# Attention of a two-layer hybrid backbone: transposed probabilities on three rotating PSUM banks, values in one piece at the head of odd steps

## The chip, the cores and the metric

The kernel runs on one core of one Trainium2 chip. The metric is the device time of one execution in microseconds, median over several; less is better. Of the core's engines, PE does the matrix products and transpositions, DVE is the vector engine, ACT the scalar engine, POOL the general-purpose one. Each engine works through its own queue in order, and semaphores tie the queues together: an instruction that waits holds up all that stand behind it in its queue.

## What is computed

Two layers, each with a SwiGLU feed-forward half step, a token mixing, and a second half step. The change touches only the attention inside the token mixing. Its core in the reference is, for 8 latent-attention heads ("mla") over all 768 tokens and 4 neighbourhood heads ("na") with a learned bias over a window:

```python
def attend(q, k, v, scale):
    s = jnp.einsum('bqhd,bkhd->bhqk', q, k).astype(jnp.float32) * scale
    p = jax.nn.softmax(s, axis=-1).astype(v.dtype)
    return jnp.einsum('bhqk,bkhd->bqhd', p, v)
...
    ya_x = blocked_attention(qa_x, jnp.concatenate([ka_c, ka_x], axis=1),
                             jnp.concatenate([va_c, va_x], axis=1), MLA_SCALE).reshape(B, S, MLA_WIDTH)
...
    yb_x = neighborhood_attention(qb_x, kb_x, vb_x, kb_c, vb_c, na_rpb, rows).reshape(B, S, NA_WIDTH)
```

There are 512 latent and 256 context tokens. A latent query attends to its latent keys (all 512, or the 256 or 384 near it in an na head) and the 256 context keys; a context query attends to the 256 context keys alone, and exists only in the first layer.

## The kernel before

Every matrix product is made of products of high and low parts in float32: an operand is split into a rounded part ("hi", written by ACT) and the rest ("lo", the difference, written by DVE or POOL). Feed-forward stages and projections keep PE busy for most of the span and are not touched. Attention is one stage in each layer, with its own loop on each engine: `attention_pe`, `attention_act`, `attention_dve` and `attention_pool`.

The unit of attention is a chunk of 128 queries of one head. Layer 0 has 72 chunks (each of 12 heads: 4 latent, 2 context), layer 1 has 48, all latent. The loops run over steps s. The work on one chunk c, and the step in which each engine's queue holds it, is:

- scores (PE, step c): matmuls into the PSUM tensor `pair[c % 2]`, lines L2086 to L2095.
- maximum (DVE, step c): one `tensor_reduce` over the scores, L2235.
- exponential (ACT, step c): from `pair` into `prob`, with the row sums, L2180.
- transposition of the probabilities (PE, step c + 2): 128x128 pieces into `pmid`, L2109. A latent chunk has two parts, the latent keys and the context keys, each with its own bank of `pmid`; a context chunk has the second part only. A part is written over only when the low half of the chunk before has been taken out of its bank.
- `pt_hi` (ACT, L2165) and `pt_lo` (DVE, L2254), both read from the transposed probabilities, step c + 2, one instruction for each part.
- values (PE, L2123 to L2136): for two chunks (2b, 2b+1) together, first two transpositions that spread the reciprocal sums, then matmuls of the values with `pt_hi` and `pt_lo`, into half of `psum2`. The first half of the matmuls stands in step 2b + 4, the second in 2b + 5, and pairs of chunks alternate between the two banks of `psum2`.
- read-out of the two chunks: a copy by ACT (L2173, step 2b + 5), a sum and a product by DVE (L2242 and L2244, step 2b + 6); the product's end is counted in `a_out`. A reciprocal (L2269) closes each even step on DVE.

ACT's queue in a step is: `pt_hi` of chunk s-2, the copy (odd s), the exponential of chunk s. Behind it, in the first three steps of a head, stands one splitting copy each for the next head (L2143). DVE's queue in a step is: maximum of chunk s, the two read-out instructions (even s), `pt_lo` of chunk s-2. PE's queue is: scores of s, both parts of the transposition of s-2, half of the values. The wait of the first half of the values lets two pairs be open:

```python
wait_if(eng, a_out, c0 // 2 + b - 1)
```

Of the kernel before, what the change touches and what calls it, by code (L numbers as in the profile page):

```python
# [29 lines left out]
P = 128  # L30
# [32 lines left out]
STATS = 6  # L63
# [138 lines left out]
def program(nc, x, c, ctx_in, c_ctx, w_mod, w_mod_rows, b_mod, w_gate, w_up, w_down, w_in, g_cq, w_q_up, g_ckv, w_kv_up,  # L202
            g_mla_q, g_mla_k, g_na_q, g_na_k, na_rpb, w_pool, pool_scale, w_out,
            k_ident, k_cos, k_sin, k_invcnt, out):
    with ExitStack() as ctx:
# [170 lines left out]
        a_latent_t, a_latent_hi, a_latent_lo = (sem(f"a_latent_{k}") for k in ("t", "hi", "lo"))  # L376
# [1661 lines left out]

        Y_ORDER = [0, 1, 6, 7, 2, 3, 4, 5]
# [23 lines left out]

        def attention_pe(eng, l):
# [6 lines left out]
            for s in range(n + 4):  # L2071
                if s == 2:
                    eng.wait_ge(v_free, TOK // P * (l + 1))
                if s < n:
                    kind, i, j, q0, keys = chunk_info(l, s)
                    g, new = att_group(l, s)
                    qh, ql, kh, kl = att_set[g % 2]
                    rows = slice(0, QK) if kind == "mla" else slice(0, 2 * NA_DIM)
                    if new:
                        eng.wait_ge(a_lo, ATT_SPLITS * l + splits(g)[0] + len(splits(g)[1]))  # L2080
                        if kind == "na":
                            eng.wait_ge(na_stacked, 48 * (NA_HEADS * l + g - MLA_HEADS + 1))
                    wait_if(eng, a_exp, c0 + s - 1)
                    for a, b in keys:
                        dst, q, d = pair[s % 2][:, a:b], slice(q0, q0 + P), moved(kind, q0, a)
                        eng.matmul(dst, qh[rows, q], kh[rows, a + d:b + d], start=True, stop=False)  # L2086
                        if kind == "mla":
                            eng.matmul(dst, qh[rows, q], kl[rows, a:b], start=False, stop=False)
                        last = eng.matmul(dst, ql[rows, q], kh[rows, a + d:b + d], start=False,
                                          stop=not (biased(l, s) and a < SEQ))  # L2090
                    if biased(l, s):
                        first, a = BIAS_FIRST[q0 // P], keys[0][0]
                        eng.wait_ge(bias_lo_done, bias_tables(l, s))
                        for table in (na_hi, na_lo):
                            last = eng.matmul(pair[s % 2][:, a:SEQ], ident_r[:, :], table[:, j, first:first + SEQ - a],  # L2095
                                              start=False, stop=table is na_lo)
                    last.then_inc(a_s, 1)
                if 2 <= s < n + 2:
                    c = s - 2
                    keys = chunk_info(l, c)[4]  # L2100
                    eng.wait_ge(a_exp, c0 + c + 1)
                    for a, b in keys:
                        part = a // SEQ
                        if part == 0:
                            wait_if(eng, a_latent_lo, latent_parts(l, c))
                        else:
                            wait_if(eng, a_ptl, c0 + c)
                        for k in range(a // P, b // P):
                            last = eng.transpose(pmid[:, k * P:(k + 1) * P], prob[:, c % 3, k * P:(k + 1) * P], ident[:, :])  # L2109
                        last.then_inc((a_latent_t, a_t)[part], 1)  # L2110
                if s >= 4:
                    b, part = (s - 4) // 2, s % 2
                    kind, i, j, q0, keys = chunk_info(l, 2 * b)
                    tiles = [[k for k in range(TOK // P) if k >= SEQ // P or 0 <= k - near(kind, x)[0] < near(kind, x)[1]]
                             for x in (q0, q0 + P)]
                    kc = sorted(set(tiles[0] + tiles[1]), key=lambda k: (k >= SEQ // P, not all(k in t for t in tiles), k))
                    if part == 0:
                        eng.wait_ge(a_ptl, c0 + 2 * b + 2)
                        wait_if(eng, a_out, c0 // 2 + b - 1)
                        eng.wait_ge(a_rsum, c0 + 2 * b + 2)  # L2120
                        for h in range(2):
                            at = (b % 2) * 512 + (2 + h) * P
                            eng.transpose(psum2[:, at:at + P], stat[:, (2 * b + h) % STATS, 2:3].broadcast_to([P, P]),  # L2123
                                          ident[:, :])
                    vals = v_both[:, :, 2 * i + j, :] if kind == "mla" else vn_both[i][:, :, j, :]
                    both = psum2[:, (b % 2) * 512:(b % 2) * 512 + 2 * P].rearrange("p (c q) -> p c q", c=2)
                    for k in kc[:len(kc) // 2] if part == 0 else kc[len(kc) // 2:]:
                        c1, c2 = [h for h in range(2) if k in tiles[h]][0], [h for h in range(2) if k in tiles[h]][-1] + 1
                        dst, slots = both[:, c1:c2, :], slice(2 * (b % 2) + c1, 2 * (b % 2) + c2)
# [365 lines left out]
```

## Time and profile before

| what | value |
|---|---|
| median of 3 runs | 2893.85 us (2892.34 to 2894.07) |
| the profiled execution, its own time | 2889.44 us |
| its span in the trace | 2887.6 us |
| PE busy over the span | 2807.2 us (97%) |
| DVE busy | 1482.7 us (51%) |
| ACT busy | 947.4 us (33%) |
| POOL busy | 263.3 us (9%) |

The trace is of one execution, which lies 4.4 us under the median of the runs. The shares are means over all stages: the feed-forward stages are PE's alone, and the attention stages, 813 to 987 us and 2334 to 2469 us of the span, are those in which PE, DVE and ACT all work most of the time.

### The profile page before, as it was taken

The numbers are of one execution on the slowest core, as the hardware profiler recorded it, in microseconds if no ns is written. First come the engines' busy times: TensorE is split into PE (matmuls) and PEld (weight loads), VectorE is DVE, ScalarE is ACT, GpSimd is POOL, SyncE is SP. The second block draws the span as 40 slices with busy tenths as digits, with TensorE's granted clock in tenths as the row PEclk, the third lists the DMA queues.
The fourth block names the chain that finished last, engine by engine and source line by source line (L and its number), as shares of the span: only waits on it lengthen the run. The fifth ranks groups of instructions, "written<-read, shape, count | busy, mean of one in ns | idle before, by whom it ended". The sixth has DMA issues, their size and how long they took to land.

```text
span 2887.6 us, 42480 instructions
## 1 busy us (share of the span) xinstructions
PE 2807.2 (97%) x16327; PEld 2646.7 (92%) x16327; DVE 1482.7 (51%) x2293; ACT 947.4 (33%) x1526; POOL 263.3 (9%) x279
## 2 busy tenths in 40 slices
PE   7999999999988899999999999999999998999999
PEld 5999999989977789999999999999998987888887
DVE  6554355455477665533553555245346587633332
ACT  3221122233388642211222322112224388532231
POOL 1000000031234210000000100000003234000000
PEclk9999999999999999999999999999999999999999
DMA  6433243223100224322442234133223201233333
GB/s 224 135 122 99 82 137 122 82 63 78 32 14 12 79 74 134 124 85 81 137 133 58 88 117 134 55 123 117 72 65 87 58 14 46 81 95 107 90 100 90
DMA packets 361092, 262.99 MB, mean 91 GB/s; under 512 B 11086, under 2 KB 339188, under 8 KB 359952
## 3 DMA queue, kind: packets, MB, share of 16 engines
q1 hardware_dynamic: 359440, 256.86, 29.5%
q10 hardware_dynamic: 896, 4.46, 0.4%
q8 instruction: 78, 1.28, 0.2%
q14 instruction: 38, 0.31, 0.0%
q0 software_dynamic: 640, 0.09, 0.0%
HBM read 255.08 MB, written 2.10 MB: 89 GB/s over the span
## 4 chain that ended last, share of the span: by engine, by line
PE 89%; ACT 4%; DVE 3%; issue 2%; POOL 1%; DMA 0%; SPq 0%; POOLq 0%; ACTq 0%; DVEq 0%
PE pair L427 24%; PE pair L428 24%; PE pair L435 24%; PE pair L1311 2%; PE pair L1313 2%; PE pair L1312 2%; PE pair L682 2%; PE pmid L2109 2%; PE pair L683 2%; PE pair L684 2%; ACT prob L2180 1%; ACT pt_hi L2165 1%; DVE pt_lo L2254 1%; PE psum L2134 1%; PE psum L2136 1%
## 5 line engine op out<-in xcount | busy, mean ns | idle before, releaser
L427 PE MATMUL pair<-h_lo,w_hi 128*128 128x384 f32 (+1 forms) x2656 | 906.4, 343 | 0.7 <-ACT sg L1102 0.4
L428 PE MATMUL pair<-h_hi,w_hi 128*128 128x384 f32 (+1 forms) x2656 | 905.4, 343 | 0.0
L427 PEld LDWEIGHTS pair<-h_lo,w_hi 128*128 128x128 f32 x2656 | 498.5, 188 | 22.8 <-issue 0.6
L428 PEld LDWEIGHTS pair<-h_hi,w_hi 128*128 128x128 f32 x2656 | 498.8, 188 | 21.3
L403 DVE TENSOR_TENSOR w_lo<-w_raw,w_hi 128x1024 fp32r<-128x1024 f32 (+1 forms) x262 | 349.0, 1332 | 324.5 <-ACT w_hi L396 321.3
L435 PE MATMUL pair<-h_hi,w_lo 128*128 128x384 f32 (+1 forms) x2656 | 513.8, 343 | 0.0
L435 PEld LDWEIGHTS pair<-h_hi,w_lo 128*128 128x128 f32 x2656 | 463.4, 188 | 20.6
L396 ACT ACTIVATE w_hi<-w_raw 128x1024 fp32r<-128x1024 f32 (+1 forms) x262 | 296.2, 1131 | 539.8 <-PE pair L435 507.4
L427 PE MATMUL pair<-s_lo,w_hi 128*128 128x384 f32 (+1 forms) x1100 | 377.7, 343 | 0.0
L428 PE MATMUL pair<-s_hi,w_hi 128*128 128x384 f32 (+1 forms) x1100 | 377.2, 343 | 0.0
L949 DVE SCALAR_TENSOR_TENSOR pmid<-mod_raw,cs_rows 128x1024 f32<-128x1024 f32 x256 | 315.3, 1232 | 74.8 <-DMA mod_raw<-in_w_mod_rows 58.1
L1133 DVE SCALAR_TENSOR_TENSOR xT<-pair,mv,xT 128x384 f32 (+4 forms) x160 | 76.5, 525 | 419.4 <-PE pair L435 415.0
L1106 ACT ACTIVATE s_hi<-sf 128x768 f32 (+3 forms) x88 | 69.8, 793 | 592.0 <-DVE sf L1160 592.0
L428 PEld LDWEIGHTS pair<-s_hi,w_hi 128*128 128x128 f32 x1100 | 206.5, 188 | 6.8
L427 PEld LDWEIGHTS pair<-s_lo,w_hi 128*128 128x128 f32 x1100 | 206.5, 188 | 6.8
L435 PE MATMUL pair<-s_hi,w_lo 128*128 128x384 f32 (+1 forms) x1100 | 209.4, 343 | 0.0
L670 POOL TENSOR_TENSOR h_lo<-nt,h_hi 128x256 fp32r<-128x256 f32 (+1 forms) x36 | 35.5, 985 | 1822.9 <-ACT nt L652 1822.9
L1102 ACT ACTIVATE sg<-pair 128x768 f32<-128x768 f32 (+1 forms) x88 | 66.9, 761 | 407.5 <-PE pair L435 407.5
L435 PEld LDWEIGHTS pair<-s_hi,w_lo 128*128 128x128 f32 x1100 | 193.8, 188 | 6.9
L1160 DVE TENSOR_TENSOR sf<-pair,sg 128x768 f32<-128x768 f32 (+1 forms) x88 | 78.4, 891 | 183.4 <-PE pair L435 178.9
L1162 DVE TENSOR_TENSOR s_lo<-sf,s_hi 128x768 f32 (+3 forms) x88 | 78.5, 892 | 91.3 <-ACT s_hi L1106 91.3
L2254 DVE TENSOR_TENSOR pt_lo<-pmid,pt_hi 128x512 fp32r<-128x512 f32 (+2 forms) x216 | 101.7, 507 | 31.4 <-ACT pt_hi L2165 29.8
(310 smaller groups left out, 3603.3 us busy)
## 6 DMA issues: line engine op xcount, KB each, us to landing
mod_raw<-in_w_mod_rows SPq DMA_DIRECT2D x64, 1024.0 KB, 4.9
w_raw<-in_w_ffn_gate SPq DMA_DIRECT2D x88, 512.0 KB, 3.8
w_raw<-in_w_ffn_up SPq DMA_DIRECT2D x88, 512.0 KB, 3.8
w_raw<-in_w_ffn_down SPq DMA_DIRECT2D x64, 704.0 KB, 4.6
w_raw<-in_w_in SPq DMA_DIRECT2D x32, 512.0 KB, 4.0
w_raw<-in_w_out SPq DMA_DIRECT2D x12, 512.0 KB, 4.2
w_raw<-in_w_q_up SPq DMA_DIRECT2D x8, 576.0 KB, 4.1
mod_first<-in_w_mod ACTq DMA_DIRECT2D x4, 1024.0 KB, 9.2
```

Of the source, the lines that this page charges most:

```text
L396: eng.activation(w_hi[:, t.odd, 0:w], raw[:, t.odd, 0:w], ACT.Copy).then_inc(w_hi_done, 1)
L403: eng.tensor_tensor(w_lo[:, t.odd, 0:w], raw[:, t.odd, 0:w], w_hi[:, t.odd, 0:w].bitcast(F32), ALU.subtract).then_inc(w_lo_done, 1)
L427: eng.matmul(dst, wh, rl, start=k == 0, stop=False)
L428: eng.matmul(dst, wh, rh, start=False, stop=False)
L435: last = eng.matmul(dst, wl, rh, start=False, stop=k == chunks - 1)
L949: eng.scalar_tensor_tensor(pmid[:, 0:D_MODEL], mod_raw[:, a, :], 1.0, cs_rows[:, j, :], ALU.mult, ALU.mult, accum_out=mod_out(v, a, j)).th ...
L1102: eng.activation(into, gate, ACT.Silu).then_inc(acc_free[o.odd], 1)
L1106: eng.activation(s_hi[:, bass.ds(i, 1), 0:w].rearrange("p a t -> p (a t)"), sf[:, 0:w], ACT.Copy).then_inc(s_hi_done, 1)
L1133: last = eng.scalar_tensor_tensor(xT[:, bass.ds(d, 1), a:b].rearrange("p a t -> p (a t)"), pair[o.odd][:, at:at + b - a], mv[:, 2, bass.ds ...
L1160: eng.tensor_tensor(into, up, gate, ALU.mult).then_inc(acc_free[(o + 1).odd], 1)
L1162: eng.tensor_tensor(s_lo[:, bass.ds(i, 1), 0:w].rearrange("p a t -> p (a t)"), sf[:, 0:w], s_hi[:, bass.ds(i, 1), 0:w].bitcast(F32).rearra ...
L2254: eng.tensor_tensor(pt_lo[:, (a + d) // P:(b + d) // P, c % 4, :], pmid[:, a:b].rearrange("p (k q) -> p k q", q=P), pt_hi[:, (a + d) // P: ...
```

## The change

The arithmetic stays the same. What moves is where results lie and the order of the queues:

- The transposed probabilities are numbered part by part, and part number x lies in one of three banks, x mod 3: the two of `pmid` and the second of `psum2`. A part may be written when the low half of the part three before has been taken.
- The values of all pairs go to the first bank of `psum2`, in one piece, at the head of odd steps (pair b in step 2b + 5). They wait until the read-out of pair b-1 is complete (`a_out` one higher than before).
- On PE the transposition of the latent part of chunk s-2 stands ahead of the scores of s, that of the context part behind them.
- On ACT the copy of the read-out stands behind the exponential, no longer ahead of it.
- On DVE `pt_lo` of the latent part stands ahead of the maximum, that of the context part behind it, and the read-out behind both.
- Three semaphores go; all parts count in `a_t`, `a_pth` and `a_ptl`.

```diff
--- before.py
+++ after.py
@@ new functions @@
+        def turn_no(l, c):
+
+            return ATT_C0[l] + c + latent_parts(l, c)
+
+        TURN_PLACES = [pmid[:, 0:512], pmid[:, 512:1024], psum2[:, 512:1024]]
+
+        def turned_at(number, a, b):
+
+            return TURN_PLACES[number % 3][:, 0:b - a].rearrange("p (k q) -> p k q", q=P)
...
+        def turn_part(eng, l, c, m):
+
+            keys = chunk_info(l, c)[4]
+            a, b = keys[m]
+            number = turn_no(l, c) + m
+            eng.wait_ge(a_exp, ATT_C0[l] + c + 1)
+            wait_if(eng, a_ptl, number - 2)
+            for k in range(a // P, b // P):
+                last = eng.transpose(turned_at(number, a, b)[:, k - a // P, :], prob[:, c % 3, k * P:(k + 1) * P], ident[:, :])
+            last.then_inc(a_t, 1)
+
+        def weigh_values(eng, l, b):
...
+            wait_if(eng, a_out, c0 // 2 + b)
+            eng.wait_ge(a_rsum, c0 + 2 * b + 2)
+            for h in range(2):
+                eng.transpose(psum2[:, (2 + h) * P:(3 + h) * P], stat[:, (2 * b + h) % STATS, 2:3].broadcast_to([P, P]),
+                              ident[:, :])
+            eng.wait_ge(a_ptl, turn_no(l, 2 * b + 2))
...
+            both = psum2[:, 0:2 * P].rearrange("p (c q) -> p c q", c=2)
+            for k in kc:
...
+            last.then_inc(a_pv, 1)
@@ attention_pe @@
             for s in range(n + 4):
                 if s == 2:
                     eng.wait_ge(v_free, TOK // P * (l + 1))
+                parts = len(chunk_info(l, s - 2)[4]) if 2 <= s < n + 2 else 0
+                if s >= 5 and s % 2:
+                    weigh_values(eng, l, (s - 5) // 2)
+                if parts == 2:
+                    turn_part(eng, l, s - 2, 0)
                 if s < n:
...
+                    attention_scores(eng, l, s)
+                if parts:
+                    turn_part(eng, l, s - 2, parts - 1)
@@ attention_act @@
-                if s >= 5 and s % 2 and s < n + 4:
-                    b = (s - 5) // 2
...
-                    eng.activation(y_f[r, i if kind == "mla" else 4 + i, q0:q0 + 2 * P], psum2[other, bank:bank + 2 * P],
-                                   ACT.Copy).then_inc(a_copied, 1)
                 if s < n:
...
-                    wait_if(eng, a_t, c0 + s - 2)
+                    if s >= 3:
+                        eng.wait_ge(a_t, turn_no(l, s - 2))
                     eng.activation(prob[:, s % 3, a:b], pair[s % 2][:, a:b], ACT.Exp, bias=stat[:, s % STATS, 0:1], accum_out=stat[:, s % STATS, 1:2]).then_inc(a_exp, 1)
+                if s >= 5 and s % 2 and s < n + 4:
+                    b = (s - 5) // 2
...
+                    eng.activation(y_f[r, i if kind == "mla" else 4 + i, q0:q0 + 2 * P], psum2[other, 0:2 * P],
+                                   ACT.Copy).then_inc(a_copied, 1)
@@ turned_lo, attention_dve @@
+            eng.wait_ge(a_pth, number + 1)
+            eng.tensor_tensor(pt_lo[:, (a + d) // P:(b + d) // P, c % 4, :], turned_at(number, a, b),
+                              pt_hi[:, (a + d) // P:(b + d) // P, c % 4, :].bitcast(F32), ALU.subtract).then_inc(a_ptl, 1)
...
             for s in range(n + 5):
+                parts = len(chunk_info(l, s - 2)[4]) if 2 <= s < n + 2 else 0
+                if parts == 2:
+                    turned_lo(eng, l, s - 2, 0)
                 if s < n:
...
                     eng.tensor_reduce(stat[:, s % STATS, 0:1], pair[s % 2][:, a:b], AX_X, ALU.max, negate=True).then_inc(a_max, 1)
+                if parts:
+                    turned_lo(eng, l, s - 2, parts - 1)
                 if s >= 6 and s % 2 == 0:
...
-                    eng.tensor_tensor(y, y, psum2[r, bank + 2 * P:bank + 4 * P], ALU.mult).then_inc(a_out, 1)
-                if 2 <= s < n + 2:
...
+                    eng.tensor_tensor(y, y, psum2[r, 2 * P:4 * P], ALU.mult).then_inc(a_out, 1)
```

PE's queue in layer 1, from the context part of chunk 2's transposition on, before; `prob_105` are the probabilities, `stat_134` the reciprocal sums, `v_both_90` the values, and in brackets stand the semaphores waited for:

```order
L2109 MATMUL pmid<-ident_136,prob_105 128x128 [waits a_ptl]
L2109 MATMUL pmid<-ident_136,prob_105 128x128
L2123 MATMUL psum2<-ident_136,stat_134 128x128 [waits a_rsum,a_out,a_ptl]
L2123 MATMUL psum2<-ident_136,stat_134 128x128
L2133 MATMUL psum2<-pt_hi_103,v_both_90 128x256
L2134 MATMUL psum2<-pt_lo_104,v_both_90 64x256 x2
L2136 MATMUL psum2<-pt_hi_103,v_both_90 128x256
L2134 MATMUL psum2<-pt_lo_104,v_both_90 64x256
L2136 MATMUL psum2<-pt_hi_103,v_both_90 128x256
L2086 MATMUL pair1<-ks_hi1_112,qs_hi1_110 128x512 [waits a_exp]
```

The same place after the change:

```order
L2108 MATMUL psum2<-ident_136,prob_105 128x128 [waits a_ptl,a_exp]
L2108 MATMUL psum2<-ident_136,prob_105 128x128
L2121 MATMUL psum2<-ident_136,stat_134 128x128 [waits a_rsum,a_out]
L2121 MATMUL psum2<-ident_136,stat_134 128x128
L2132 MATMUL psum2<-pt_hi_103,v_both_90 128x256 [waits a_ptl]
L2133 MATMUL psum2<-pt_lo_104,v_both_90 64x256 x2
L2135 MATMUL psum2<-pt_hi_103,v_both_90 128x256
L2133 MATMUL psum2<-pt_lo_104,v_both_90 64x256
L2135 MATMUL psum2<-pt_hi_103,v_both_90 128x256
L2133 MATMUL psum2<-pt_lo_104,v_both_90 64x256
L2135 MATMUL psum2<-pt_hi_103,v_both_90 128x256
L2133 MATMUL psum2<-pt_lo_104,v_both_90 64x256
```

The first half of the values (3 of 6 key tiles) stood between this transposition and the scores of chunk 5; now all six tiles stand there, the context part goes to `psum2`'s second bank, and the latent transposition of chunk 3 follows before those scores.

DVE's queue in steps 5 and 6 of layer 1, before; L2235 is the maximum, L2242 and L2244 the read-out:

```order
L2235 TENSOR_REDUCE stat_134<-pair1 128x1 [waits a_s]
L2254 TENSOR_TENSOR pt_lo_104<-pmid,pt_hi_103 128x4x128 [waits a_latent_hi]
L2254 TENSOR_TENSOR pt_lo_104<-pmid,pt_hi_103 128x2x128 [waits a_pth]
L2235 TENSOR_REDUCE stat_134<-pair0 128x1 [waits a_s]
L2242 TENSOR_TENSOR y_f_91<-y_f_91,psum2 64x256 [waits a_copied]
L2244 TENSOR_TENSOR y_f_91<-y_f_91,psum2 64x256 [waits a_added]
L2254 TENSOR_TENSOR pt_lo_104<-pmid,pt_hi_103 128x4x128 [waits a_latent_hi]
L2254 TENSOR_TENSOR pt_lo_104<-pmid,pt_hi_103 128x2x128 [waits a_pth]
L2269 RECIPROCAL stat_134<-stat_134 128x2 [waits a_exp]
```

and after, where L2261 is the maximum, L2243 `pt_lo`, L2270 and L2272 the read-out:

```order
L2243 TENSOR_TENSOR pt_lo_104<-pmid,pt_hi_103 128x4x128 [waits a_pth]
L2261 TENSOR_REDUCE stat_134<-pair1 128x1 [waits a_s]
L2243 TENSOR_TENSOR pt_lo_104<-pmid,pt_hi_103 128x2x128 [waits a_pth]
L2243 TENSOR_TENSOR pt_lo_104<-psum2,pt_hi_103 128x4x128 [waits a_pth]
L2261 TENSOR_REDUCE stat_134<-pair0 128x1 [waits a_s]
L2243 TENSOR_TENSOR pt_lo_104<-pmid,pt_hi_103 128x2x128 [waits a_pth]
L2270 TENSOR_TENSOR y_f_91<-y_f_91,psum2 64x256 [waits a_copied]
L2272 TENSOR_TENSOR y_f_91<-y_f_91,psum2 64x256 [waits a_added]
L2284 RECIPROCAL stat_134<-stat_134 128x2 [waits a_exp]
```

In each step one `pt_lo` instruction has moved from behind the maximum to ahead of it, and the read-out from behind the maximum to behind both `pt_lo`.

ACT's queue in steps 5 and 6 of layer 1, before; L2165 is `pt_hi`, L2173 the copy, L2180 the exponential, L2143 a splitting copy of the next head:

```order
L2165 ACTIVATE pt_hi_103<-pmid 128x4x128 [waits a_latent_t]
L2165 ACTIVATE pt_hi_103<-pmid 128x2x128 [waits a_t]
L2173 ACTIVATE y_f_91<-psum2 64x256 [waits a_pv]
L2180 ACTIVATE prob_105,stat_134<-pair1,stat_134 128x768 [waits a_t,a_max]
L2143 ACTIVATE ks_hi0_108<-k_f_80 96x768
L2165 ACTIVATE pt_hi_103<-pmid 128x4x128 [waits a_latent_t,a_pv]
L2165 ACTIVATE pt_hi_103<-pmid 128x2x128 [waits a_t]
L2180 ACTIVATE prob_105,stat_134<-pair0,stat_134 128x768 [waits a_t,a_max]
```

and after, where L2179 is `pt_hi`, L2187 the exponential, L2193 the copy:

```order
L2179 ACTIVATE pt_hi_103<-pmid 128x4x128 [waits a_t]
L2179 ACTIVATE pt_hi_103<-pmid 128x2x128 [waits a_t]
L2187 ACTIVATE prob_105,stat_134<-pair1,stat_134 128x768 [waits a_t,a_max]
L2193 ACTIVATE y_f_91<-psum2 64x256 [waits a_pv]
L2160 ACTIVATE ks_hi0_108<-k_f_80 96x768
L2179 ACTIVATE pt_hi_103<-psum2 128x4x128 [waits a_t,a_pv]
L2179 ACTIVATE pt_hi_103<-pmid 128x2x128 [waits a_t]
L2187 ACTIVATE prob_105,stat_134<-pair0,stat_134 128x768 [waits a_t,a_max]
```

The copy has moved behind the exponential; the rest stands as before.

## Rows read from the trace of the kernel before

**Rows 1.** Attention stages: stretch, length, busy us of PE, PEld, DVE, ACT, POOL; clock, DMA.

```profile
813.20:987.40 174.20, 147.14 (x1056) 132.58 (x1056) 135.88 (x299) 142.29 (x337) 64.80 (x35) 0.98 0.11 30
2333.80:2469.40 135.60, 121.52 (x881) 111.63 (x882) 108.81 (x219) 112.64 (x253) 55.26 (x35) 0.99 0.12 34
```

**Rows 2.** Waits of PE for `pt_lo`, layer 0 and layer 1: us in total, times, longest.

```profile
PE pmid L2109 <- DVE pt_lo L2254: 20.8, 31, 1.9
...
PE pmid L2109 <- DVE pt_lo L2254: 3.1, 10, 0.5
```

**Rows 3.** Timeline, two steps in layer 1: start us, duration us, engine, line, operation.

```profile
2350.68 0.94 DVE L2235 TENSOR_REDUCE stat<-pair 128x1 f32<-128x768 f32 x1
...
2351.10 0.36 PE L2134 MATMUL psum<-pt_lo,v_both 128*64 128x256 f32 x1
...
2351.89 0.40 PE L2086 MATMUL pair<-ks_hi,qs_hi 96*128 96x512 f32 x1
...
2352.12 0.38 ACT L2173 ACTIVATE y_f<-psum 64x256 f32<-64x256 f32 x1
...
2352.53 0.90 ACT L2180 ACTIVATE prob<-pair,stat 128x768 f32<-128x768 f32 x1
...
2352.94 0.82 PE L2109 MATMUL pmid<-ident,prob 128*128 128x128 f32 x6
...
2353.14 0.96 DVE L2235 TENSOR_REDUCE stat<-pair 128x1 f32<-128x768 f32 x1 [0.26 <-PE pair L2089]
...
2353.60 0.38 PE L2123 MATMUL psum<-ident,stat 128*128 128x128 f32 x2
...
2354.52 0.40 PE L2086 MATMUL pair<-ks_hi,qs_hi 96*128 96x512 f32 x1
...
2355.79 0.94 DVE L2235 TENSOR_REDUCE stat<-pair 128x1 f32<-128x768 f32 x1
```

**Rows 4.** Timeline at the start of attention in layer 0, with waits in brackets.

```profile
814.55 2.00 DVE L2235 TENSOR_REDUCE stat<-pair 128x1 f32<-128x768 f32 x2
...
815.61 0.90 ACT L2180 ACTIVATE prob<-pair,stat 128x768 f32<-128x768 f32 x1 [2.37 <-DVE stat L2235]
...
819.45 1.02 DVE L2254 TENSOR_TENSOR pt_lo<-pmid,pt_hi 128x512 fp32r<-128x512 f32 x2 [0.43 <-ACT pt_hi L2165]
...
820.29 0.85 PE L2109 MATMUL pmid<-ident,prob 128*128 128x128 f32 x6 [0.56 <-DVE pt_lo L2254]
...
820.95 0.87 ACT L2165 ACTIVATE pt_hi<-pmid 128x512 fp32r<-128x512 f32 x2 [0.39 <-PE pmid L2109]
...
821.58 0.69 DVE L2254 TENSOR_TENSOR pt_lo<-pmid,pt_hi 128x512 fp32r<-128x512 f32 x1 [0.18 <-ACT pt_hi L2165]
```

**Rows 5.** Groups by shape, 813 to 988 us: count, busy us, mean ns, idle before.

```profile
L2254 DVE TENSOR_TENSOR pt_lo<-pmid,pt_hi 128x256 fp32r<-128x256 f32 x80 | 32.7, 417 | 5.6 <-ACT pt_hi L2165 4.8
...
L2244 DVE TENSOR_TENSOR y_f<-y_f,psum 64x256 f32<-64x256 f32 x35 | 14.6, 418 | 1.2
...
L2235 DVE TENSOR_REDUCE stat<-pair 128x1 f32<-128x256 f32 x24 | 9.9, 411 | 1.4 <-PE pair L2089 1.4
...
L2235 DVE TENSOR_REDUCE stat<-pair 128x1 f32<-128x640 f32 x8 | 6.6, 822 | 2.7 <-PE pair L2095 2.7
...
L2143 ACT ACTIVATE ks_hi<-k_f 96x768 fp32r<-96x768 f32 x7 | 5.8, 833 | 0.0
```

**Rows 6.** PE and its granted clock (fourth number) in short stretches, and one timeline row.

```profile
920.00:930.00 10.00, 6.90 (x43) 0.83 0.27 61
950.00:960.00 10.00, 7.33 (x50) 0.83 0.38 97
2440.00:2450.00 10.00, 8.15 (x53) 0.83 0.09 20
...
926.00:927.00 1.00, 1.00 (x6) 0.50 0.07 16
...
925.75 1.50 PE L2109 MATMUL pmid<-ident,prob 128*128 128x128 f32 x6 [1.67 <-DVE pt_lo L2254]
```

More of the change, by code:

```diff
@@ new lines, in turn_part @@
+        def turn_part(eng, l, c, m):
[8 more added lines that the diff above has]
+        def weigh_values(eng, l, b):
+            c0 = ATT_C0[l]
+            kind, i, j, q0, keys = chunk_info(l, 2 * b)
+            tiles = [[k for k in range(TOK // P) if k >= SEQ // P or 0 <= k - near(kind, x)[0] < near(kind, x)[1]]
+                     for x in (q0, q0 + P)]
+            kc = sorted(set(tiles[0] + tiles[1]), key=lambda k: (k >= SEQ // P, not all(k in t for t in tiles), k))
+            wait_if(eng, a_out, c0 // 2 + b)
[4 more added lines that the diff above has]
+            eng.wait_ge(a_ptl, turn_no(l, 2 * b + 2))
+            vals = v_both[:, :, 2 * i + j, :] if kind == "mla" else vn_both[i][:, :, j, :]
+            both = psum2[:, 0:2 * P].rearrange("p (c q) -> p c q", c=2)
+            for k in kc:
+                c1, c2 = [h for h in range(2) if k in tiles[h]][0], [h for h in range(2) if k in tiles[h]][-1] + 1
+                dst, slots = both[:, c1:c2, :], slice(2 * (b % 2) + c1, 2 * (b % 2) + c2)
+                ph, pl = pt_hi[:, k, slots, :], pt_lo[:, k, slots, :]
+                first, end = k == kc[0], k == kc[-1]
+                if first:
+                    eng.matmul(dst, vals[:, k, :], ph, start=True, stop=False)
+                last = eng.matmul(dst[0:V_DIM], vals[:, k, 0:V_DIM], pl, start=False, stop=False)
+                if not first:
+                    last = eng.matmul(dst, vals[:, k, :], ph, start=False, stop=end)
+            last.then_inc(a_pv, 1)
@@ L2073, in attention_pe @@
                     eng.wait_ge(v_free, TOK // P * (l + 1))
-                if s < n:
[L2075 to L2097, printed above, removed]
@@ L2098, in attention_pe @@
-                if 2 <= s < n + 2:
[L2099 to L2129, printed above, removed]
-                        ph, pl = pt_hi[:, k, slots, :], pt_lo[:, k, slots, :]
-                        first, end = k == kc[0], k == kc[-1]
-                        if first:
-                            eng.matmul(dst, vals[:, k, :], ph, start=True, stop=False)
-                        last = eng.matmul(dst[0:V_DIM], vals[:, k, 0:V_DIM], pl, start=False, stop=False)
-                        if not first:
-                            last = eng.matmul(dst, vals[:, k, :], ph, start=False, stop=end)
-                    if part:
-                        last.then_inc(a_pv, 1)
@@ L2158, in attention_act @@
                     kind, _, _, q0, keys = chunk_info(l, c)
[L2159 removed]
+                    for number, (a, b) in enumerate(keys, turn_no(l, c)):
                         d = moved(kind, q0, a)
[L2161 to L2174 removed]
+                        eng.wait_ge(a_t, number + 1)
+                        eng.activation(pt_hi[:, (a + d) // P:(b + d) // P, c % 4, :], turned_at(number, a, b),
+                                       ACT.Copy).then_inc(a_pth, 1)
                 if s < n:
@@ L2238, in attention_dve @@
                     kind, i, j, q0, _ = chunk_info(l, 2 * b)
[L2239 removed]
+                    r = slice(j * 64, j * 64 + 64)
                     y = y_f[r, i if kind == "mla" else 4 + i, q0:q0 + 2 * P]
                     eng.wait_ge(a_copied, c0 // 2 + b + 1)
[L2242 removed]
+                    eng.tensor_tensor(y, y, psum2[r, 0:2 * P], ALU.add).then_inc(a_added, 1)
                     eng.wait_ge(a_added, c0 // 2 + b + 1)
[L2244 to L2257 removed]
+                    eng.tensor_tensor(y, y, psum2[r, 2 * P:4 * P], ALU.mult).then_inc(a_out, 1)
                 if n + 1 <= s < n + 3:
```

59 lines of the change are left out of this document (32 added, 27 removed).

## The prediction, as put on record

> **What bounds the kernel now.** The change touches attention alone, so I read first how long that stage is and who works in it, from the busy times of stretches: 174.2 us in layer 0 and 135.6 us in layer 1, with PE busy 147.1 and 121.5 us, DVE and ACT some 8 tenths of the time each [rows 1]. The reader is to see that three engines are nearly full, so that the order of their queues decides, and that PE has at most 27 + 14 = 41 us to give. The waits come next: PE waited 20.8 + 3.1 us for the low half that frees a bank of `pmid` [rows 2]. This is what a third bank can take away.
>
> Then the timeline of one settled pair of steps in layer 1 [rows 3]. PE's scores take 2351.89 to 2352.94 = 1.05 us, both parts of the transposition 2352.94 to 2353.60 = 0.66, the first half of the values 2353.60 to 2354.52 = 0.92, the second half 2351.10 to 2351.89 = 0.79. A pair of steps is 2 x 1.05 + 2 x 0.66 + 1.71 = 5.13 us of PE, and the maxima of like steps, 2350.68 and 2355.79, lie 5.11 apart. So PE bounds layer 1 here. This works because of the order of the other queues: while DVE takes the maximum of chunk s, ACT makes `pt_hi` of s-2; while ACT takes the exponential of s, DVE makes `pt_lo` of s-2. Read-out has a whole pair of steps to spare, since two banks hold values.
>
> **The change, part by part.** No matmul or transposition is added or dropped, and no DMA moves. What changes is who waits for whom, so I follow one pair of steps (s odd, then s+1) of an all-latent mla head through the new queues. Each length is a row.
>
> The ring begins where the product that ends the read-out of pair b-1 is done on DVE; the values of pair b stand behind it.
>
> 1. DVE's end to PE's start, 0.15: a `pt_lo` of two parts starts at 819.45, its first part lasts 0.69 as at 821.58, and PE starts at 820.29 [rows 4].
> 2. Values in one piece: 1.71 in two pieces, each with a start of its own; I take 1.65 [rows 3].
> 3. Start of the latent transposition of s-2 to the start of `pt_hi`, 820.29 to 820.95: 0.66 [rows 4].
> 4. `pt_hi` to `pt_lo`, 820.95 to 821.58: 0.63 [rows 4].
> 5. `pt_lo` now stands ahead of the maximum of s: two parts take 1.02 [rows 4], the second alone 0.42 [rows 5], so 0.60.
> 6. Maximum 0.94 [rows 3]; to ACT 0.10, from about 815.5 (half of 2.00 from 814.55) to 815.61 [rows 4]; exponential 0.90 [rows 3].
> 7. Copy of the read-out, now behind the exponential: 2352.12 to 2352.53, 0.41 [rows 3].
> 8. Only now does ACT come to `pt_hi` of s-1: 0.63 to `pt_lo`, then 0.60 and the maximum of s+1, 0.94.
> 9. `pt_lo` of the context part 0.42, sum and product 0.42 each and 0.03 between them [rows 5].
>
> Sum: 0.15 + 1.65 + 0.66 + 0.63 + 0.60 + 0.94 + 0.10 + 0.90 + 0.41 + 0.63 + 0.60 + 0.94 + 0.42 + 0.87 = 9.5 us for a pair of steps, against 5.11. Two things make it. The `pt_lo` ahead of the maximum makes ACT and DVE take turns: step to step the ring maximum, exponential, `pt_hi`, `pt_lo` is 0.94 + 0.10 + 0.90 + 0.63 + 0.60 = 3.2 us, or 6.8 for a pair with the copy. And the single values bank puts the read-out, the values and a transposition into the same ring, for another 2.7. PE does 5.1 us of work in the 9.5 and stands for 4.4 in one piece, between the context transposition of s-1 and the values. The third bank does its work (PE never waits for `pt_lo` of the part three before), but that wait is no longer the one that counts.
>
> Layer 0 has 6 chunks a head, 4 latent and 2 context, thus three kinds of pairs. Where s-2 is a context chunk, scores stand right behind the values, and their start to the maximum's is 1.25 (2351.89 to 2353.14) [rows 3] in place of steps 3 to 5 (1.89): 8.9 us. Where s is latent, s+1 context and the values of two context chunks (2 of 6 key tiles, some 0.75 us), the last maximum is 0.41 [rows 5]: 8.1. Where s is a context chunk, its maximum is 0.41 and the chain stays on DVE through `pt_lo`, the next maximum, `pt_lo` and read-out: 6.8. A head gives 23.8, eight heads 190. The na heads have parts of 256 or 384, maxima of 0.82 or less [rows 5] and 5 key tiles: the same addition gives about 7.9 for a latent pair and 20.5 for a head of layer 0, 82 for four. Once a head one splitting copy of 0.83 [rows 5] lies behind the copy in an odd step and so in the ring: 11 x 0.8 = 9. Less one pair, since 36 values make 35 intervals, and with 11 us to fill and empty the pipe, layer 0 comes to 190 + 82 + 9 - 8 + 11 = 284 us against 174.2 [rows 1]: +110. Layer 1, with 16 mla and 8 na pairs: 16 x 9.5 + 8 x 7.9 + 9 - 8 + 11 = 227 against 135.6: +91. Together +201.
>
> **PE's clock.** In the trace before, the granted clock fell three times within attention (0.83 over 10 us), each time after a few us in which PE stood more than it worked; it then was 0.50, that is 1.2 instead of 2.4 GHz, for some 3.3 us, and six transpositions took 1.50 instead of 0.85 us [rows 4, 6]. After the change PE stands for 3 to 5 us in nearly every one of 60 pairs. So I expect a fall in most. One costs at most half of 3.3 us, 1.65, if all of it lies on values, transposition and scores, which are 3.1 us at the head of the ring; some will lie in the standstill, and for shorter pairs less counts. I take 1.2 for 52 pairs: +62. The ends are 0 (no fall) and the clock low throughout: then values, transposition and scores take twice as long, some 2.5 us a pair over all kinds, +150.
>
> The Trainium skill ("TensorE: Matmul & The Clock Gate", section "HAM oscillation — how this bites in real kernels") has a rule that speaks against this change: bursts of matmuls with idle gaps between them can start slow each time. By that rule the fall comes in every pair, by three falls alone it could stay the exception; the sums are those of the forecast and of the first rival below, and this case's trace agrees as far as its three falls go.
>
> Against the profiled execution of 2889.4 us: 2889.4 + 201 + 62 = 3152. That execution lies 4.4 under the median, so **3157 us**.
>
> **The rivals.**
> - *The clock stays up.* The same ring without falls: 2893.8 + 201 = 3095. For it: in most of the stage before, short waits did no harm. Against it: the three falls followed standstills of the length that now comes every pair [rows 6]. 0.17.
> - *The clock stays low.* Work at half speed lengthens PE's bursts, which may be what brings the clock back; if not, 3095 + 150 = 3245. After each fall before, it came back. 0.09.
> - *Only the turn-taking of ACT and DVE binds*, the read-out ends in time. A latent mla pair is 6.8; the three kinds of layer 0 come to about 14.4 by the same rows, 4.8 a pair against 174.2 / 36 = 4.8 now [rows 1], so only the 16 mla pairs of layer 1 pay, 1.7 each, 27 us: 2921. Against it: the product stands behind a maximum whose scores are the last large work ahead of the values on PE, so it can't be early. 0.08.
> - *Faster.* The wait for a bank goes and nothing takes its place: 2893.8 - 24 = 2870. It decides at 5.1 us: if the ring from one product to the next were under that, PE would go on unhindered. The sum is 9.5, and an error of nearly half of it in rows read directly is hard to see. 0.03.
> - *Nothing changes*, because the old waits merely shift: within 6 us of 2894. 0.02. A rest of 0.01 lies between.
>
> **How the numbers follow.** The forecast has 0.60. The range takes in its own spread (0.7 to 1.65 us a fall, 0.2 us either way in a ring) and the rivals of the clock: 3075 to 3250. Below it lie the 0.08, 0.03 and 0.02 and little else. All cases but the last two are slower; 0.2% (6 us) is about what a measurement of this kernel can tell from no change. Faster 0.03, same 0.02, slower 0.95.
>
> **What would show it.** Attention of about 315 us in layer 0 and 260 in layer 1, all else as before. PE waiting some 4 us ahead of the spreading transpositions (L2121) for the product L2272, 60 times less a few, 180 to 260 us in all; no wait of note at L2108 for `pt_lo`. ACT's `pt_hi` ahead of DVE's maximum in the chain, which now runs through DVE and ACT for over half of the stage. Maxima of like steps 9.5 us apart in layer 1, more where the clock is 0.50; mean clock of the stage near 0.8. The forecast is wrong if the wait at L2121 is short, if maxima lie 7 us apart (then the values are not in the ring), or if the clock is 1.0 throughout.

## The result and the profile after

The changed kernel takes 3165.72 us (median of 4 runs, 3164.95 to 3166.42) against 2893.1 us before (4 runs, 2889.57 to 2894.07): 1.0945 times as long, 95% interval 1.0926 to 1.0964. The forecast was 3157, in a range of 3075 to 3250. The profiled execution took 3166.41 us.

From the page of the changed kernel, PE's busy time, the slices (busy tenths of PE, tenths of full clock) and the row of the costliest groups that is new there (mean ns, then the idle time ahead of it and what ended it):

```profile
PE 2903.6 (92%) x16327; PEld 2738.4 (87%) x16327; DVE 1486.3 (47%) x2293; ACT 961.2 (30%) x1526; POOL 260.7 (8%) x279
...
PE   7999999999766689999999999999999765799999
...
PEclk9999999999877889999999999999999978899999
...
L2121 PE MATMUL psum<-ident,stat 128*128 128x128 f32 x120 | 34.9, 385 | 211.9 <-DVE y_f L2272 211.9
```

PE has the same 16327 matmuls and is busy 96 us longer than before, DVE and ACT nearly as long as before (+3.6 and +13.8 us). That is the sign of a slower clock on PE alone, and the third line has it in two places: the attention stages. L2121, the transpositions that open the values, now stands behind 211.9 us of idle time ended by L2272, the product of the read-out.

The attention stages by busy time, which answer to [rows 1]; after each stretch and its length come busy us and instructions of PE, PEld, DVE, ACT and POOL, then clock and DMA:

```profile
812.50:1135.10 322.60, 201.69 (x1056) 185.36 (x1057) 139.93 (x302) 149.32 (x336) 64.29 (x35) 0.77 0.06 16
2486.10:2747.50 261.40, 162.79 (x890) 148.92 (x891) 112.25 (x224) 121.25 (x255) 54.62 (x35) 0.80 0.07 19
```

Layer 0 takes 322.6 us in place of 174.2, with the clock at 0.77 in place of 0.98. The second stretch holds 9 matmuls more than its counterpart in [rows 1]; up to the same 881st matmul layer 1 takes some 259 us in place of 135.6, with the clock at 0.80 in place of 0.99. To compare the settled part of both layers, here are PE's rows from the first values to the last, of the kernel before and then of the changed one (length, PE busy, clock):

```profile
823.10:986.30 163.20, 139.03 (x1008) 0.98 0.11 28
...
2343.40:2466.00 122.60, 110.26 (x814) 0.99 0.12 32
```

```profile
823.10:1133.80 310.70, 192.54 (x1007) 0.76 0.06 15
2496.50:2740.70 244.20, 148.13 (x814) 0.80 0.06 16
```

That is +147.5 and +121.6 us, 269 of the 277 us by which the span grew. The waits of PE in the two stages, which answer to [rows 2] (total us, times, longest):

```profile
PE psum L2121 <- DVE y_f L2272: 118.1, 35, 5.3
...
PE pmid L2108 <- DVE pt_lo L2243: 0.2, 1, 0.2
...
PE psum L2121 <- DVE y_f L2272: 93.8, 23, 5.8
```

The wait for `pt_lo` fell from 20.8 us to 0.2 in layer 0: the three banks do what they are for. In its place stand 58 waits of 3.7 us on average, in every pair but the first of each layer.

One pair of steps in layer 1, which answers to [rows 3] (start, duration; in brackets the idle time ahead):

```profile
2595.73 0.60 ACT L2179 ACTIVATE pt_hi<-psum 128x512 fp32r<-128x512 f32 x1 [3.96 <-PE psum L2108]
...
2598.33 0.90 ACT L2187 ACTIVATE prob<-pair,stat 128x768 f32<-128x768 f32 x1 [0.39 <-DVE stat L2261]
...
2599.34 0.38 ACT L2193 ACTIVATE y_f<-psum 64x256 f32<-64x256 f32 x1
2599.62 0.83 ACT L2160 ACTIVATE ks_hi<-k_f 96x768 fp32r<-96x768 f32 x1
2600.48 0.60 ACT L2179 ACTIVATE pt_hi<-pmid 128x512 fp32r<-128x512 f32 x1
...
2601.11 0.69 DVE L2243 TENSOR_TENSOR pt_lo<-pmid,pt_hi 128x512 fp32r<-128x512 f32 x1 [2.48 <-ACT pt_hi L2179]
2601.72 0.95 DVE L2261 TENSOR_REDUCE stat<-pair 128x1 f32<-128x768 f32 x1
2602.58 0.41 DVE L2243 TENSOR_TENSOR pt_lo<-psum,pt_hi 128x256 fp32r<-128x256 f32 x1
...
2602.91 0.40 DVE L2270 TENSOR_TENSOR y_f<-y_f,psum 64x256 f32<-64x256 f32 x1
2603.35 0.41 DVE L2272 TENSOR_TENSOR y_f<-y_f,psum 64x256 f32<-64x256 f32 x1
...
2603.82 0.69 PE L2121 MATMUL psum<-ident,stat 128*128 128x128 f32 x2 [4.58 <-DVE y_f L2272]
...
2606.86 0.71 PE L2108 MATMUL pmid<-ident,prob 128*128 128x128 f32 x4
2607.67 0.60 ACT L2179 ACTIVATE pt_hi<-pmid 128x512 fp32r<-128x512 f32 x1 [3.46 <-PE pmid L2108]
```

Read it as a ring. The exponential is followed by the copy, a splitting copy and only then by `pt_hi`; `pt_lo` follows 0.63 us later, then the maximum, the second `pt_lo`, sum and product, and PE starts 0.06 us behind the product after 4.58 us of standing. The values then take 2603.82 to 2606.86 = 3.04 us, where the prediction took 1.65. Why, is seen in PE's stretches of 1 us (busy us, then the clock) over the same time:

```profile
2599.00:2600.00 1.00, 0.23 (x3) 1.00 0.00 0
2600.00:2601.00 1.00, 0.00 (x0) 1.00 0.00 0
2601.00:2602.00 1.00, 0.00 (x0) 1.00 0.00 0
2602.00:2603.00 1.00, 0.00 (x0) 1.00 0.00 0
2603.00:2604.00 1.00, 0.18 (x1) 0.83 0.00 0
2604.00:2605.00 1.00, 1.00 (x6) 0.50 0.00 0
2605.00:2606.00 1.00, 1.00 (x6) 0.50 0.00 0
2606.00:2607.00 1.00, 1.00 (x6) 0.50 0.00 0
2607.00:2608.00 1.00, 1.00 (x8) 0.96 0.00 0
```

The clock stays at 2.4 GHz through most of the 4.58 us of standing, is 1.2 GHz just as the values begin, and is back at 2.4 GHz when they are over.

### The profile page after: what moved, and what is told of

Read it like the earlier page. It is cut to its first block, busy times and chain, and to the rows that moved or that the text cites. A ratio compares the mean times of both kernels' runs of the same rounds, so it can differ in the third digit from the quotient of the medians.

```text
span 3164.6 us, 42570 instructions
## 1 busy us (share of the span) xinstructions
PE 2903.6 (92%) x16327; PEld 2738.4 (87%) x16327; DVE 1486.3 (47%) x2293; ACT 961.2 (30%) x1526; POOL 260.7 (8%) x279
## 4 chain that ended last, share of the span: by engine, by line
PE 85%; DVE 7%; ACT 5%; issue 2%; DMA 0%; POOL 0%; SPq 0%; POOLq 0%; ACTq 0%; DVEq 0%
PE pair L426 21%; PE pair L427 21%; PE pair L434 21%; DVE stat L2261 2%; DVE pt_lo L2243 2%; PE pair L1310 2%; PE pair L1312 2%; PE pair L1311 2%; PE psum L2133 2%; PE pair L681 2%; PE pair L682 2%; PE pair L683 2%; PE psum L2135 1%; ACT pt_hi L2179 1%; PE psum L2121 1%
## 5 line engine op out<-in xcount | busy, mean ns | idle before, releaser
L2121 PE MATMUL psum<-ident,stat 128*128 128x128 f32 x120 | 34.9, 385 | 211.9 <-DVE y_f L2272 211.9
L2121 PEld LDWEIGHTS psum<-ident,stat 128*128 128x128 f32 x120 | 15.0, 175 | 226.3 <-DVE y_f L2272 226.3
```

What stands on the lines that cost most here:

```text
L2121: eng.transpose(psum2[:, (2 + h) * P:(3 + h) * P], stat[:, (2 * b + h) % STATS, 2:3].broadcast_to([P, P]), ident[:, :])
```

## The experiments

The changes are small edits of the changed kernel. Four questions: is the loss in the bank of the values, in the queues of DVE and ACT, in PE's order, or in the clock; and is there an order that keeps the third bank and loses nothing? The kernel before took 2894.3 us beside the runs with two banks, the old queues, the maximum first and 28 products, and 2890 us (median) beside the others, so times of the two groups can be compared to some 4 us. A time that is given without a number of runs is of a single run, whose own spread isn't known.

**Two banks for the values again** (and two for the transposed parts), all queues as changed:

```diff
-        TURN_PLACES = [pmid[:, 0:512], pmid[:, 512:1024], psum2[:, 512:1024]]
+        TURN_PLACES = [pmid[:, 0:512], pmid[:, 512:1024]]
...
-            wait_if(eng, a_ptl, number - 2)
+            wait_if(eng, a_ptl, number - 1)
...
-            wait_if(eng, a_out, c0 // 2 + b)
+            wait_if(eng, a_out, c0 // 2 + b - 1)
...
-            both = psum2[:, 0:2 * P].rearrange("p (c q) -> p c q", c=2)
+            both = psum2[:, (b % 2) * 512:(b % 2) * 512 + 2 * P].rearrange("p (c q) -> p c q", c=2)
```

> The changed kernel with the PSUM banks as before: the parts of the transposed probabilities alternate over the two banks of pmid, the values of pairs alternate over the two banks of psum2 and wait only for the read-out of the pair before last. All queue orders stay as changed. Theory A (two rings, one through the read-out and one by ACT and DVE taking turns): the ring through the read-out is gone, the turn-taking stays at some 6.8 us for an all-latent pair of steps in layer 1, and with PE hardly standing its clock stays near 1.0: 2905 to 2945 us. Rival B (the queue orders alone make the loss, and the values would be late with two banks too): above 3080 us.

It took 2970.0 us. The ring through the read-out is gone: rival B is out. But the time is 25 us above what theory A allowed. The clock was not near 1.0 either, as theory A had it, but at 0.93 in both layers (PE's busy time and clock):

```profile
812.50:1020.00 207.50, 159.76 (x1058) 0.93 0.10 26
2385.00:2550.00 165.00, 122.96 (x811) 0.93 0.09 24
```

PE's longest wait in layer 0 was 2.7 us here, so standstills well under 4 us bring falls too. The maxima in layer 1, of two steps of a pair and the first of the next:

```profile
2405.61 0.95 DVE L2261 TENSOR_REDUCE stat<-pair 128x1 f32<-128x768 f32 x1
...
2408.71 0.95 DVE L2261 TENSOR_REDUCE stat<-pair 128x1 f32<-128x768 f32 x1
...
2411.11 0.95 ACT L2198 ACTIVATE na_hi<-na_tt 128x896 fp32r<-128x896 f32 x1
...
2413.18 0.95 DVE L2261 TENSOR_REDUCE stat<-pair 128x1 f32<-128x768 f32 x1
```

3.10 and 4.47 us; without the 0.86 that a copy for the bias (L2198) holds ACT, 6.7 for a pair, as worked out (6.8). That is the shortest kind: the openings of the values of the mla heads in layer 1 lie mostly 6.6 to 8.1 us apart. What I had left out, beside the clock, is that ACT is in this ring in every step, so that the splitting copies of even steps count too, and that in layer 0, with two banks, PE waits for `pt_lo`:

```profile
PE pmid L2108 <- DVE pt_lo L2243: 44.4, 44, 2.7
```

How the 25 us divide among the three no run shows.

**The old queues of ACT and DVE**, with the changed banks and PE's changed order:

```diff
@@ attention_dve @@
-                if parts == 2:
-                    turned_lo(eng, l, s - 2, 0)
                 if s < n:
...
-                if parts:
-                    turned_lo(eng, l, s - 2, parts - 1)
                 if s >= 6 and s % 2 == 0:
...
+                if parts == 2:
+                    turned_lo(eng, l, s - 2, 0)
+                if parts:
+                    turned_lo(eng, l, s - 2, parts - 1)
```

(and on ACT the copy ahead of the exponential)

> The changed kernel with the queue orders of ACT and DVE as before (copy ahead of the exponential; on DVE maximum, read-out, then both pt_lo), but still one bank for the values, three for the transposed probabilities, and PE's queue as changed. Theory A: the read-out then follows the maximum at once, and the ring is read-out, values, transposition and scores of s, transposition and scores of s+1, maximum: some 7.0 us for an all-latent pair in place of 5.1, PE stands about 2 us a pair before L2121: 2930 to 2990 us, with a clock of 0.95 or more. Rival C (the single bank alone makes the loss whatever the orders): above 3080 us. Rival B (the orders alone): 2900 or below.

2972.4 us, as theory A has it; the rivals B and C are out. PE still waits for the read-out in every pair, but less long. Its wait in layer 0:

```profile
PE psum L2121 <- DVE y_f L2268: 50.9, 35, 3.0
```

The openings of the values lie mostly 6.9 to 7.1 us apart in the mla heads of layer 1, where 7.0 was expected and the changed kernel has 10.7 to 12.7. The clock was 0.92 in the stage of layer 0, under the 0.95 that was expected, and 0.97 in that of layer 1.

**The maximum first**, both `pt_lo` behind it, nothing else:

```diff
-                if parts == 2:
-                    turned_lo(eng, l, s - 2, 0)
                 if s < n:
...
+                if parts == 2:
+                    turned_lo(eng, l, s - 2, 0)
                 if parts:
                     turned_lo(eng, l, s - 2, parts - 1)
```

> The changed kernel with one thing undone on DVE: the maximum stands ahead of both pt_lo instructions again; the read-out stays behind them, banks and the other queues as changed. Theory A: the ring keeps the read-out, both pt_lo of s-1 and the exponential, and loses one maximum-behind-pt_lo: 8.4 in place of 9.5 us an all-latent pair, so some 40 to 70 us less than the changed kernel: 3095 to 3125. Rival D (that pt_lo ahead of the maximum is the cause of nearly all): under 2960.

3111.0 us, 55 under the changed kernel, in the range of theory A; rival D is out. The place of `pt_lo` is a term of the ring, not the cause of nearly all.

**PE's order alone**: the edits for two banks and for the old queues together, so that little but PE's queue differs from the kernel before (the transposed parts still take the two banks by number and not by kind, which differs in layer 0 alone).

> The kernel before with PE's queue alone as changed: values in one piece at the head of odd steps, the latent transposition of s-2 ahead of the scores of s. Banks (two for the transposed parts, two for the values) and the queues of ACT and DVE as before. Theory A (rings): with two banks a transposition waits for the pt_lo of the chunk before, which stands behind the maximum on DVE, and the scores now stand behind that transposition; in the even steps there are no values to cover it. Ring over a latent pair: 2 x (0.45 transposition + 1.25 to the maximum + 0.94 + 0.69 pt_lo + 0.15) + 0.87 read-out = 7.8 us in place of 5.1, with values inside the wait: 2950 to 3030 us, and PE waits for pt_lo at L2108, 60 us or more in all. Rival F (PE's order matters little as long as two banks hold the values): 2885 to 2910.

2953.3 us, 63 above the kernel before: rival F is out. PE's idle time ahead of the transpositions that `pt_lo` ended, over both layers:

```profile
DVE pt_lo L2243: 80.6, 71
```

That is 80.6 us where the kernel before has 23.9 [rows 2], 57 more of the 63. The openings of the values in the mla heads of layer 1 lie 7.6 to 7.9 us apart, where 7.8 was expected.

The parts of the change can now be set side by side, all with PE's new order: 2953 with neither; 2970 with the new queues alone; 2972 with the new banks alone; 3166 with both. Each adds 17 to 19 us (13 to 15 if each is taken against the kernel before beside it), both together 213. The lengths of a pair in the mla heads of layer 1 say why: 7.6 to 7.9 us with neither, 6.6 to 8.1 with the queues, 6.9 to 7.1 with the banks, all over PE's 5.1. Each of these three has a ring of its own, and in layer 1 the new one is no longer than the one that it replaces. In layer 0 it is somewhat longer: from first to last values 180 us with neither, 194 with the queues, 210 with the banks, 311 with both. With both, the pieces lie in one ring, and the clock comes on top.

**The clock.** Small products that nobody reads are put on PE in the standstill ahead of the values:

```diff
+            eng.wait_ge(a_exp, c0 + min(2 * b + 4, n_chunks(l)))
+            for x in range(28):
+                eng.matmul(pair[1][:, 0:P], ident_r[:, :], ident_r[:, :], start=True, stop=True)
             wait_if(eng, a_out, c0 // 2 + b)
```

> The changed kernel with 28 small products (128x128 moving 128 columns, results never read) put on PE ahead of the values of each pair, where PE stands; they wait only for an exponential that is over by then, and are to take about 3 of the 4 us of the standstill. Theory A: the rings stay, but the granted clock stays at 1.0 in the attention stages, and the time falls by the price of the clock, 62 us as predicted: about 3100 (3080 to 3125). Rival E (the clock costs nothing since the low stretches lie in the standstill): 3160 or more.

3121.3 us with 1680 more products than the changed kernel: 45 us less, at the upper end of theory A's range and under the 62 forecast. Rival E is out. The clock was 0.96 and 0.98 from the first values to the last in the two layers. With a nearly steady clock the ring can be measured bare. Two openings of the values in layer 1:

```profile
2552.37 0.43 PE L2124 MATMUL psum<-ident,stat 128*128 128x128 f32 x2 [1.25 <-DVE y_f L2275]
...
2558.01 3.34 PE L2120 MATMUL pair<-ident_r 128*128 128x128 f32 x28 [0.37 <-ACT prob L2190]
2558.38 0.95 ACT L2201 ACTIVATE na_hi<-na_tt 128x896 fp32r<-128x896 f32 x1
...
2562.70 0.43 PE L2124 MATMUL psum<-ident,stat 128*128 128x128 f32 x2 [1.36 <-DVE y_f L2275]
```

10.33 us, of which the copy for the bias is 0.86: 9.47, where the prediction had 9.5. A pair with no such copy in the ring needs no subtraction:

```profile
2532.80 0.43 PE L2124 MATMUL psum<-ident,stat 128*128 128x128 f32 x2 [1.10 <-DVE y_f L2275]
...
2542.15 0.43 PE L2124 MATMUL psum<-ident,stat 128*128 128x128 f32 x2 [0.37 <-DVE y_f L2275]
```

9.35 us, and PE still waits for the product at its end, so the added products don't set its length. In layer 0 they do in every third pair, as the wait there is short (7.9 us in place of 6.9 with fewer products), which is what the next two runs are about.

> As the run called filler, with 18 in place of 28 added products, so that they fit into the shorter standstills of layer 0 too. In the first of the two the added work overran them (the waits for the read-out fell to 12 us in 12 places in layer 0). Theory A: clock 0.97 or more in attention, rings bare, 3095 to 3110 us, some 60 under the changed kernel. Rival (the overrun cost nothing, and the clock's price is the 45 us that filler showed): 3118 or more, or the clock falls again because the rest of the standstill is too long: 3130 or more.

3139.8 us: the second rival. Eighteen products leave too much of the standstill, and the clock falls again, in layer 1 nearly as low as without them (0.80); the row is that of layer 1:

```profile
2490.00:2710.00 220.00, 178.81 (x1131) 0.82 0.07 18
```

> As the run called filler (28 added products ahead of the values), but 18 in the third of the pairs of layer 0 whose standstill is the shortest, where 28 lengthened the pair from some 6.8 to 7.9 us. Theory A: clock at 0.95 or more in attention as with 28, and 8 to 15 us less than that run: 3106 to 3114. Rival (fewer products let the clock fall again in those pairs, as 18 everywhere did): 3120 or more.

3109.6 us, as theory A has it. Its stretches up to the last values, in layer 0 from the first values on, with the clock at 0.96 and 0.97:

```profile
831.10:1106.00 274.90, 243.06 (x1868) 0.96 0.07 17
2470.00:2684.00 214.00, 189.79 (x1441) 0.97 0.07 19
```

Layer 0 has 274.9 us against 310.7; in layer 1 the first values lie at 2467.9, so it has 216.1 against 244.2. The clock costs at least 35.8 + 28.1 = 64 us there. The whole kernel gained 57 only (54 against the kernel before beside each), since the first values of layer 0 come 8 us later with the added products (831.1 in place of 823.1).

**Orders meant to be better than both.** The first two keep the banks and the queues of ACT and DVE as they were before (but for the numbering of the two banks in layer 0, as above), and put the half of the values elsewhere on PE. The edit on PE, against the changed kernel:

```diff
...
-                if s >= 5 and s % 2:
-                    weigh_values(eng, l, (s - 5) // 2)
-                if parts == 2:
-                    turn_part(eng, l, s - 2, 0)
                 if s < n:
                     attention_scores(eng, l, s)
+                if s >= 4:
+                    weigh_values(eng, l, (s - 4) // 2, s % 2)
+                if parts == 2:
+                    turn_part(eng, l, s - 2, 0)
                 if parts:
                     turn_part(eng, l, s - 2, parts - 1)
```

> A version of the kernel before meant to be better than both: banks and the queues of ACT and DVE as before, the values in two halves as before, but on PE the half of the values stands between the scores of s and the transposition of s-2, so that 0.8 us of work lies ahead of the wait for the bank. Theory A: the wait for pt_lo (20.8 + 3.1 us) goes, no ring reaches 5.1 us: 2870 to 2892 us. Rival G (the transposition comes 0.8 us later, pt_hi and with it the exponential come later and the next scores wait for the exponential instead): 2893 to 2930.

2910.7 us (5 runs), 1.0067 times the kernel before, 1.0054 to 1.0081: a little slower, in the range of rival G and above that of theory A, but not by its mechanism alone. ACT did wait longer for the transposition, 34.6 us in place of 23.6 in layer 0. But the wait for `pt_lo` did not go either, it moved to the first matmul of the values, which needs it too, and remained in part at the transposition. The two rows, of layer 0:

```profile
PE psum L2133 <- DVE pt_lo L2245: 20.0, 26, 2.2
PE pmid L2108 <- DVE pt_lo L2245: 5.7, 11, 1.2
```

With the half between the latent and the context part:

> As values_between, but the half of the values stands between the latent and the context part of the transposition. Theory A: the wait for the latent bank stays as before, only that for the context bank is covered: 2885 to 2900 us, no clear difference from the kernel before. Rival G (a later context part delays pt_hi and the exponential behind it): 2900 to 2930.

2899.4 us (6 runs), 1.003 times, 1.0018 to 1.0042: in theory A's range, a little slower than the kernel before.

The last keeps the changed banks, takes DVE's old queue, and lets PE take the values at the end of odd steps:

```diff
-                if s >= 5 and s % 2:
-                    weigh_values(eng, l, (s - 5) // 2)
-                if parts == 2:
-                    turn_part(eng, l, s - 2, 0)
                 if s < n:
                     attention_scores(eng, l, s)
+                if parts == 2:
+                    turn_part(eng, l, s - 2, 0)
                 if parts:
                     turn_part(eng, l, s - 2, parts - 1)
+                if s >= 5 and s % 2:
+                    weigh_values(eng, l, (s - 5) // 2)
```

> The changed kernel's banks (three for the transposed parts, one for the values) with queues laid out so that no ring reaches PE's own work: PE takes scores of s, both parts of the transposition of s-2, and in odd steps then the values of the pair in one piece; DVE takes the maximum, the read-out, both pt_lo, as before; ACT keeps the copy behind the exponential. Theory A: the ring through the read-out is values 1.65, scores 1.05 and 0.2 to the maximum 0.94, sum and product 0.87, 0.15 = 4.9 us a latent pair, under PE's 5.1, and no transposition waits for the pt_lo of the chunk before: 2865 to 2888 us. Rival H (one bank for the values costs time in any order, since ACT or DVE are late as well): 2894 to 2950.

2903.1 us (5 runs), 1.0042 times, 1.0028 to 1.0056. It lies in the range of rival H; theory A's 2865 to 2888 was missed. The same banks as in the changed kernel, and 263 us less by order alone: the ring through the read-out is now nearly covered. But it doesn't beat the kernel before: the openings of the values in the mla heads of layer 1 lie 5.6 to 5.9 us apart, not 5.1. In layer 0 PE's longest waits are

```profile
PE pmid L2108 <- DVE pt_lo L2243: 12.5, 14, 1.3
PE psum L2108 <- DVE pt_lo L2243: 7.6, 9, 1.5
PE psum L2121 <- DVE y_f L2268: 6.3, 13, 1.7
```

The waits for `pt_lo` are the larger part, 20.1 us, against 6.3 for the single bank of the values. On DVE `pt_lo` of even steps stands behind the read-out; that this is what makes it too late for three banks is read from the queue, and no run tests it. None of the three beat the kernel before; what would is open.

## Why the prediction was right

- *The ring and its length.* Forecast: 9.5 us for an all-latent pair at full clock. Measured with the clock held up: 9.47, and 9.35 in a pair that needs no subtraction. The kinds of layer 0 were 8.9 + 0.8 for the splitting copy, 8.1 and 6.8 us; with fitted products they measure 9.4 to 9.6, 7.9 and 6.7 to 6.9. The sums over the layers from first to last values, 281 - 8 = 273 and 224 - 8 = 216 us, stand against 274.9 and 216.1. So the sum is right term by term and not by errors that cancel, though it leaves out the copies for the bias, 1.7 us a layer, so that an agreement within 2 us is a little better than it deserves. The terms were read directly from rows of the kernel before, and the only skill was to follow the order of all three queues at once.
- *What PE waits for.* Forecast: the product L2272, in nearly every pair, about 4 us, 180 to 260 us in all, and no wait of note for `pt_lo` at L2108. Measured: 211.9 us in 58 waits, 3.7 on average; 0.2 us for `pt_lo` at L2108 in layer 0 and none in layer 1.
- *The clock.* Forecast 1.2 us a pair, +62 in all, stage mean near 0.8. Measured: 0.77 and 0.80, and 64 us by the stretches of the run with fitted products. The fall was told from three single falls before [rows 6]; that it would come in most pairs was an inference from the length of the standstill, and the runs with 28 and with 18 products show that the standstill is what brings it. One premise was misread: the three falls before did not follow standstills of 3 to 5 us. The waits just ahead of them are 1.67, 1.93 and 2.26 us, with little work around them. The error made the fall seem to need more than it does, so it did no harm here, but it hid that the two-bank kernel would lose clock too (0.93).
- *The stages.* Forecast about 315 and 260 us; measured 322.6 and some 259. The forecast total of 3157 lies 9 us (0.3%) under the 3165.7. Part of it are the copies for the bias, 0.86 us each and in the ring in two pairs a layer, which the sum had left out. And 277.0 - 269.1 = 7.9 us of the growth lie outside the stretches from first to last values, where the forecast had none; what causes them is open. That the total came within 0.3% is in part luck: the price of a fall was an estimate between 0.7 and 1.65 us.
- *Two things were wrong beside the main line.* The rival "only the turn-taking binds" was priced at 2921, with layer 0 paying nothing; the run with two banks for the values took 2970. The sum left out every second splitting copy and the clock (0.93), and the run has in addition PE's waits for `pt_lo` (44.4 us in layer 0), since it gives up the third bank, which the rival kept. And the prediction gives PE's new order no price: alone it costs some 60 us, because the scores, and with them the maximum that DVE takes ahead of `pt_lo`, stand behind a transposition that waits for `pt_lo`. Three banks hide that, which is why it didn't spoil the sum.

## What to carry to other kernels

Where three in-order queues are all nearly full, add the round trip from one read-out to the next instruction that needs its bank, through every instruction that stands ahead in each queue, and hold it against the busiest engine's work for the same round; a buffer taken from one place to serve another pays only if both round trips stay under it. Costs of such edits don't add: here two changes of under 20 us each made 213 together, since alone each put one ring in the place of another of much the same length, and together they met in one. A standstill that comes in every round was dearer here than its own length, for the work right behind it ran at half the clock, and that work was on the path.

## What was not expected of the hardware

The regularity of the clock: with nearly 4 us of standing in a round, the fall to 1.2 GHz came right at the head of the burst in the pair shown, and the values, 1.68 us at full clock (2552.37 to 2554.05 in the run with 28 products), took 3.04. Products that fill most of the standstill (28 of them, 3.3 us) kept the clock at 0.96 to 0.98 from first to last values; 18 of them (2.2 us) only lifted that of the stages from 0.77 and 0.80 to 0.89 and 0.82. Work that nobody reads made the changed kernel 45 us faster, and 57 us where its amount was fitted to the standstills.
